# A hybrid encoder layer on one Trainium2 core: the end of mixing in another order, the first gathers inside it, the second expert's loads behind them, the first low part on VectorE, and constant products in TensorE's waits

## The reference, cut to what matters

```
h = concat([meta, x])                       # 16 meta rows + 1024 rows, D = 1024
u = rmsnorm(h);  z = u @ w_in
mixed = concat([rwkv7_mix(z_a), retention_mix(z_b)])
h = h + mixed @ w_out
u = rmsnorm(h, norm_ffn)
# hier_moe(u):
group = top1(softmax(u @ w_rg + b_rg))                  # 4 groups
e1, e2 = top2(softmax(u @ w_re + b_re)[group])          # 8 experts in a group
row_tok[dest] = token of each slot, expert by expert, blocks of 128 rows
for each block (xb = u[row_tok], e):
    hid = silu(xb @ w_gate[e]) * (xb @ w_up[e])         # 1024 -> 512
    y = hid @ w_down[e]                                 # 512 -> 1024
out = rmsnorm(h + weighted sum of the two y rows of a token)
```

## Time and profile before

| what | value |
|---|---|
| median of 3 runs | 1520.82 us (1520.25 to 1533.48) |
| the profiled execution's own time | 1519.76 us |
| its span, first to last instruction | 1517.8 us |
| TensorE busy | 1395.5 us, 92% |
| VectorE busy | 1037.2 us, 68% |
| ScalarE busy | 707.8 us, 47% |
| GpSimd busy | 576.0 us, 38% |
| mean granted TensorE clock | 0.968 |
| read from HBM, written | 295.47 MB, 68.98 MB |

### The profile page before, as it was taken

One profiled execution on the slowest core, in us unless ns is written; L12 is line 12 of the kernel. 1 busy time (PEld: TensorE's weight loads), 2 busy tenths in 40 slices (PEclk: granted clock), 3 DMA queues, 4 the chain that ended last, 5 costly groups with the idle time before them and its releaser, 6 DMA issues. The chain is left out here.

```text
span 1517.8 us, 33023 instructions
## 1 busy us (share of the span) xinstructions
PE 1395.5 (92%) x14368; PEld 1235.1 (81%) x14368; DVE 1037.2 (68%) x1184; ACT 707.8 (47%) x695; POOL 576.0 (38%) x203
## 2 busy tenths in 40 slices
PE   5999999999999899999999749999999999999990
PEld 5989899999988789888898637888888888888870
DVE  5456655544203866776767558999899898777757
ACT  5533442212212412212122137777777777777752
POOL 2001101000000300000000058777877878999985
PEclk9999999999998999999999869999999999999995
DMA  5136555643418324434242369999999999999968
GB/s 211 57 126 189 166 163 165 207 129 112 128 57 279 109 87 134 127 108 141 74 133 72 115 255 423 409 405 407 407 411 404 409 403 410 413 414 414 412 245 324
DMA packets 125369, 366.26 MB, mean 241 GB/s; under 512 B 11680, under 2 KB 79264, under 8 KB 113200
## 3 DMA queue, kind: packets, MB, share of 16 engines
q1 hardware_dynamic: 112432, 318.34, 56.5%
q0 software_dynamic: 6912, 25.17, 4.8%
q10 hardware_dynamic: 5904, 20.97, 3.4%
HBM read 295.47 MB, written 68.98 MB: 240 GB/s over the span
## 5 line engine op out<-in xcount | busy, mean ns | idle before, releaser
L1111 PE MATMUL ps<-u_hi,w_hi 128*128 128x352 f32 (+1 forms) x720 | 237.9, 330 | 4.9 <-DVE u_lo L761 4.9
L1111 PE MATMUL ps<-u_lo,w_hi 128*128 128x352 f32 (+1 forms) x720 | 233.7, 325 | 0.0
L1111 PE MATMUL ps<-u_hi,w_lo 128*128 128x352 f32 (+1 forms) x720 | 232.7, 323 | 0.0
L2534 POOL TENSOR_TENSOR down_lo<-down_raw,down_hi 128x1024 fp32r<-128x1024 f32 x31 | 150.9, 4869 | 62.2 <-ACT down_hi L2603 62.2
L2534 POOL TENSOR_TENSOR gate_lo<-gate_raw,gate_hi 128x1024 fp32r<-128x1024 f32 x32 | 161.3, 5040 | 23.1 <-ACT gate_hi L2603 23.1
L2701 DVE TENSOR_TENSOR down_lo<-down_raw,down_hi 128x3072 fp32r<-128x3072 f32 x31 | 125.6, 4050 | 41.8 <-ACT down_hi L2603 41.8
L1111 PEld LDWEIGHTS ps<-u_hi,w_hi 128*128 128x128 f32 x720 | 137.4, 191 | 11.8 <-issue 5.8
L2701 DVE TENSOR_TENSOR gate_lo<-gate_raw,gate_hi 128x3072 fp32r<-128x3072 f32 x32 | 130.7, 4084 | 14.6 <-ACT gate_hi L2603 14.3
L2701 DVE TENSOR_TENSOR up_lo<-up_raw,up_hi 128x3072 fp32r<-128x3072 f32 x32 | 128.6, 4017 | 15.1 <-ACT up_hi L2603 14.8
L1501 POOL TENSOR_TENSOR mix_stat<-mix_stat,minus_half 128x4 f32<-128x4 f32 x8 | 8.2, 1025 | 341.2 <-DVE mix_stat L1800 341.2
L1111 PEld LDWEIGHTS ps<-u_hi,w_lo 128*128 128x128 f32 x720 | 137.4, 191 | 0.0
(11 more groups left out here) (444 smaller groups left out, 3120.8 us busy)
## 6 DMA issues: line engine op xcount, KB each, us to landing
down_raw<-in_moe_w_down SPq DMA_DIRECT2D x32, 2048.0 KB, 10.9
gate_raw<-in_moe_w_gate SPq DMA_DIRECT2D x31, 2048.0 KB, 10.5
up_raw<-in_moe_w_up SPq DMA_DIRECT2D x31, 2048.0 KB, 9.6
tm_rows<-tm_stage SPq DMA_DIRECT2D x32, 512.0 KB, 3.5
y_slots<-y_out ACTq DMA_DIRECT2D x31, 512.0 KB, 11.5
w_raw<-in_w_in SPq DMA_DIRECT2D x30, 512.0 KB, 4.1
tm<-tm_rows SPq DMA_DIRECT2D x36, 256.0 KB, 3.2
y_slots<-zero SPq DMA_DIRECT2D x15, 512.0 KB, 5.3
```

Source lines behind the costliest of these rows:

```text
L1111: mm = pe.matmul(z_of(n, r_), w[n % 3][:, k_, :], a[:, k_, c0:c1], start=(k_ == 0 and i == 0), stop=(k_ == KD - 1 and i == 2))
L2534: pool.tensor_tensor(lo[e % 2][:, cut:, :], raw[e % 2][:, cut:, :], hi[:, cut:, :].bitcast(F32), ALU.subtract).then_inc(sem(f"{name}_lo2_r ...
```

## The change

All edits are in the mixing block's tail, at the head of the experts' block, and in TensorE's waits within the experts' products.

```diff
+KEPT = ("consts_loaded", "x_rows_loaded0", "x_rows_loaded1", "w_gate_loaded1")   # not cleared
+        second_raw = [... offset=weights_at + (2 + i) * MATRIX ...]   # gate, up of expert 1
+        first_gate_lo = ... offset=weights_at     # in the bytes of first_raw[0]
+        first_gate_hi = ... offset=weights_at + 6 * MATRIX
+        first_x = [... offset=weights_at + 9 * MATRIX + b * 4 * D ...]
# mixing, SyncE, the end
                 first_weights(0, "moe_w_gate")
                 first_weights(1, "moe_w_up")
-                store_h2(NTX)
-                store_u2(NTX)
+                sp.wait_ge(sem("proj1_done"), NTX)
+                sp.wait_ge(sem("proj0_done"), NTX)
                 sp.wait_ge(sem("h2_stored"), 16 * NTX)
                 sp.wait_ge(sem("u2_stored"), 16 * NTX)
+                sp.wait_ge(sem("x_rows_loaded0"), 16)
+                sp.dma_start(second_raw[0][:], d["moe_w_gate"][1]).then_inc(sem("w_gate_loaded1"), 16)
# mixing, GpSimd, the end
                 rstd_h(NTX)
+                pool.wait_ge(sem("u2_stored"), 16 * NTX)
+                pool.wait_ge(sem("slot_row_ready"), 1)
+                for b in range(2):
+                    pool.indirect_dma_start(first_x[b][:], ... slot_row[:, b:b + 1] ...)
# mixing, ScalarE, the end
                 mean_square(NTX)
+                act.dma_start(h2_dram[...], h2[:]).then_inc(sem("h2_stored"), 16)
+                act.wait_ge(sem("first_weights_loaded"), 16 * 4)
+                act.wait_ge(sem("proj1_done"), NTX)
+                act.activation(first_gate_hi[:], first_raw[0][:], ACT.Copy).then_inc(sem("first_gate_hi_ready"), 1)
+                act.wait_ge(sem("u2_ready"), NTX)
+                act.dma_start(u2_dram[...], u2[:]).then_inc(sem("u2_stored"), 16)
# mixing, VectorE: a_gate for all tiles
+                    dve.wait_ge(sem("tm_gate_loaded"), 16 * n)
+                    tt(y[:], y[:], toks(n, "gate"), ALU.mult, "a_gated")
                     dve.wait_ge(sem("rstd_a"), n)
                     tt(heads(y[:]), heads(y[:]), per_head(stat[:, 2, :]), ALU.mult, "a_normed")
                     dve.wait_ge(sem("a_normed"), n)
-                    dve.wait_ge(sem("tm_gate_loaded"), 16 * n)
-                    tt(y[:], y[:], toks(n, "gate"), ALU.mult, "a_gated")
# mixing, VectorE, the end
                 a_variance(NTX)
-                choose_group(NTX - 1)
                 a_gate(NTX)
                 low_a(NTX)
+                choose_group(NTX - 1)
                 choose_first(NTX - 1)
                 choose_second(NTX - 1)
                 residual(NTX, 0)
-                rows(NTX - 2, 0)
+                residual(NTX, 1, LAST_HALF)
+                rows(NTX - 2, ROWS_BANK)
                 ranks(NTX - 1, 0)
                 entries(NTX - 1)
-                rows(NTX - 1, 0)
-                residual(NTX, 1)
                 h_variance(NTX)
-                norm(NTX)
                 logits_of(NTX)
                 choose_group(NTX)
                 choose_first(NTX)
                 choose_second(NTX)
+                norm(NTX)
+                rows(NTX - 1, ROWS_BANK)
                 ranks(NTX, 0)
                 entries(NTX)
-                rows(NTX, 0)
-                dve.tensor_copy(slot_row[:, 0:NE], slot_sum[:]).then_inc(sem("slot_row_ready"), 1)
+                dve.tensor_tensor(slot_row[:, 0:NE], slot_sum[:], ps[:, ROWS_BANK, 128:128 + NE], ALU.add).then_inc(sem("slot_row_ready"), 1)
                 (count copied, slot_row_ready 2 waited for)
+                dve.wait_ge(sem("first_gate_hi_ready"), 1)
+                dve.tensor_tensor(first_gate_lo[:], first_raw[0][:], first_gate_hi[:].bitcast(F32), ALU.subtract)
# mixing, TensorE, the end
                 ret_rows_0(NTX)
+                ret_rows_1(NTX, LAST_HALF)        # ends with keep_busy(..., 2) for tile 8
                 turn_y(NTX)
                 rwkv_rows_0(NTX)
+                rwkv_rows_1(NTX, LAST_HALF)
+                turn_h2_0(NTX)                    # waits for the first half of h2 only
+                rows_of(NTX - 2, ROWS_BANK)
                 rank(NTX - 1, 0)
-                rows_of(NTX - 2, 0)
-                ret_rows_1(NTX)
-                rows_of(NTX - 1, 0)
-                rwkv_rows_1(NTX)
-                turn_h2(NTX)
+                turn_h2_1(NTX)
                 route(NTX)                        # waits for h2_t1 only ahead of its matmul 4 of 8
+                rows_of(NTX - 1, ROWS_BANK)
+                keep_busy(pe, ps, cst, 4, 4)
                 rank(NTX, 0)                      # its count product now behind its other two
+                keep_busy(pe, ps, cst, 4, 1)
-                rows_of(NTX, 0)
+                rows_of(NTX, ROWS_BANK)
+                keep_busy(pe, ps, cst, 4, 6)
# experts, SyncE, the start
-                    sp.wait_ge(sem("x_rows_loaded0"), 16)
-                    sp.dma_start(gate_raw[1][:], one(wg_v, 1))...
+                    for name in ("gate_hi_ready", "gate_lo_ready", "gate_lo2_ready"):
+                        sp.sem_inc(sem(name), 1)
+                    sp.dma_start(down_raw[0][:], one(wd_v, 0))...
                     sp.dma_start(up_raw[1][:], one(wu_v, 1))...
-                    for b in range(2):
-                        sp.dma_start(down_raw[b][:], one(wd_v, b))...
+                    sp.dma_start(down_raw[1][:], one(wd_v, 1))...
# experts, GpSimd, the start
-                    bring_x(0)
-                    bring_x(1)
-                    low("gate", 0)
# experts, ScalarE: high("gate", 0, 0) gone; VectorE: low("gate", 0, 0) gone, turned_x(0) first
# experts, TensorE
-                        pe.wait_ge(sem("gate_lo2_ready"), e + 1)      # ahead of gate(e)
+                        rest = (GATE_CUT, lambda: pe.wait_ge(sem("gate_lo2_ready"), e + 1))
+                        # the same wait, now inside the product, ahead of k = 6 of 8
+                        # up: the same; down, last_down: ahead of k = 3 of 4 of the first half
                     turn_x(0, 0)
+                    keep_busy(pe, ps, env["cst"], 3, 2)
```

More of the change, by code:

```diff
@@ L169, in free_sems @@
         def free_sems():
-            names = [n for n in sems if n != "consts_loaded"]
+            names = [n for n in sems if n not in KEPT]
             nc.clear_and_free_semaphores([sems.pop(n) for n in names])
@@ L1281, in project @@
     return first_at, fm1, m_fm
+LAST_HALF = 1
+COUNT_BANK, ROWS_BANK = 2, 3
+GATE_CUT, DOWN_CUT = 6, 3
 def mix(nc, d, env):
@@ L2092, in m_state, with project @@
                     mm.then_inc(sem("m_products_done"), 1)
-                def project(c, hi, lo, at_, first, last):
+                def project(c, hi, lo, at_, first, last, bank=None):
                     cols = slice(c * 512, (c + 1) * 512)
@@ L2409, in dispatch_and_experts @@
             down_hi_last = nc.alloc_sbuf_tensor_at("down_hi_last", [P, KE, D], F32R, offset=h_at)
-            matrices = {"gate": (gate_raw, gate_lo, gate_hi, 6), "up": (up_raw, up_lo, up_hi, 6),
-                        "down": (down_raw, down_lo, down_hi, 3)}
-            x_rows = [sb(f"x_rows{b}", D) for b in range(2)]
+            matrices = {"gate": (gate_raw, gate_lo, gate_hi, GATE_CUT), "up": (up_raw, up_lo, up_hi, GATE_CUT),
+                        "down": (down_raw, down_lo, down_hi, DOWN_CUT)}
+            assert h_at == rows_at + 6 * MATRIX and nc.sbuf_base == rows_at + 9 * MATRIX
+            sb("first_rows", 2, D)
+            x_rows = env["first_x"]
             x_hi, x_lo = (tile(s, n, [P, KD, P], F32R) for n in ("x_hi", "x_lo"))
@@ L2832, in extra_rows @@
                         dve.wait_ge(sem("extra_rows_ready"), 1)
+                    turned_x(0)
                     weights_begun()
-                    low("gate", 0, 0)
-                    turned_x(0)
                     for e in range(NE):
@@ L2947, in last_down, with down @@
                     def last_down(e, b):
-                        for name in ("hid_hi", "hid_lo", "down_hi", "down_lo", "down_lo2"):
+                        for name in ("hid_hi", "hid_lo", "down_hi", "down_lo"):
                             pe.wait_ge(sem(f"{name}_ready"), e + 1)
-                        product(0, x_hi, x_lo, down_hi_last, down_lo[b], KE, slice(0, 512)).then_inc(sem("last_half_done"), 1)
+                        rest = (DOWN_CUT, lambda: pe.wait_ge(sem("down_lo2_ready"), e + 1))
+                        product(0, x_hi, x_lo, down_hi_last, down_lo[b], KE, slice(0, 512), rest).then_inc(sem("last_half_done"), 1)
                         product(1, x_hi, x_lo, down_hi_last, down_lo[b], KE, slice(512, D)).then_inc(sem("down_done"), 1)
-                    def down(e, b, between=None):
+                    def down(e, b, between=None, whole=False):
                         pe.wait_ge(sem("hid_hi_ready"), e + 1)
@@ L2994, in more @@
                         turn_x(e, 0)
-                        gate(e, 0)
-                        up(e, 0)
+                        gate(e, 0, whole=True)
```

(3 more changed lines are left out.)

96 lines of the change are left out of this document (61 added, 35 removed).

## The result

| | median us | runs | ratio to before, 95% interval |
|---|---|---|---|
| before | 1525.25 (1520.25 to 1533.48) | 10 | |
| after | 1513.81 (1509.04 to 1517.60) | 10 | 0.9926 [0.9910, 0.9943] |

The change is 0.74% faster; the forecast was 1512.0 us in 1504 to 1517, 0.6% faster. The profiled execution of after took 1514.83 us, its span is 1513.0, its mean clock 0.976.

What follows compares the result with a forecast made beforehand. TensorE sets the pace once the experts run, so the start of up(2), fed by mixing's tail and the weights' stream, counts: 1519.76 - 8.8 = 1511.0, plus 1.1 to the median gives 1512.0 us, range 1504 to 1517.

Steps and rivals of the forecast that it cites:

- Part 1: Mixing's tail: slot list at 873.1 and count at 873.3, against 882.0 and 882.18; the tail 8.9 us shorter.
- rival C: Mixing's tail stays at half clock in part, giving 5.5 to 6.5 us; 1514.5 to 1516 us; chance 0.13.
- The gate factor: Mixing's tail: computed ahead of the power -1/2, it was booked at 0.15 us, bounds 0 and 0.7.
- Part 2: Mixing's end: first gather held behind VectorE's low-part subtraction, landing at 882.3; stream of weights 7.3 us earlier; chance 0.50.
- Rival A: Mixing's end: gather ahead of the subtraction, landed 878.0, stream 11.6 us earlier; 1507.7 us; chance 0.28.
- The block's end: End of mixing: waits for SyncE; with 2.0 us of barrier the experts' block begins at 884.7.
- Part 3: Expert 0's first product: gate(0) at 889.5 instead of 894.09, taking 5.6 instead of 7.3 us, done 6.2 earlier.
- Down 0 ahead of up 1: SyncE's queue of loads: up 1 lands third, at about 900, costing nothing, at most 1 us.
- Part 4: Third expert: gate matrix 2 lands at 916.5, GpSimd's quarter no longer counts, up(2) at 930.7, 8.8 us earlier.
- The same rhythm: Experts from up(2) on: unchanged rhythm of 18 us per expert.
- Part 5: Moved waits in the experts' loop: gain nothing, satisfied waits cost nothing; bounds 0 and 0.12 us each.
- rival D: Experts' loop: 31 x 3 waits inside products at 0.12 us each cost 11.2, making 1523.2 us; chance 0.03.

Runs made afterwards that it cites:

- one gather: The changed kernel with only the first gather issued in mixing, the second first on GpSimd in the experts' block; 1512.60 us, ratio 0.9918.
- the first experiment: The changed kernel with the low part of the first gate matrix back at the head of the experts' block; 1509.18 us, ratio 0.9895.
- up 1 first: The changed kernel with up matrix 1 requested ahead of down matrix 0 again; 1511.42 us, ratio 0.9917.

## Why the prediction was right, and where its terms were off

The sign and the mechanism were right: a shorter tail and a stream of weights that starts earlier. That the time came within 2 us is partly luck. The prediction took 8.8 us off 1520.8, the median of three runs of before; ten runs gave 1525.25, 4.4 us more, and the change gained 11.4 by the medians and 7.1 to 7.4 behind y0. As a ratio it told 0.9942, just inside the interval of 0.9910 to 0.9943. The prediction's own times are put behind y0 here by taking 845.17 off.

- **Part 1, the tail.** Forecast 8.9 us shorter with the count at 28.1; measured 29.0 after and in two kernels more, 27.4 in seven with the same tail. The two values are some eight rwkv matmuls at half clock, or none, with the same instructions ahead: rival C in small, at 1.6 us and not the 2.5 and more that it was priced at. "I take full clock from here on" was right in seven of ten profiles. The gate factor gave 0.42 us (turn at 6.91 against 7.33), not 0.15.
- **Part 2, gather second.** Held, by the forecast's mechanism: subtraction 4.43 (4.5 forecast), gather ending 1.01 behind it (0.9), landing 3.4 later (3.5), gate matrix 1 requested at 37.9 (37.1). What was called a choice "by a hair" was none: the prediction let the gather start as soon as list and store were there, but it started 0.77 us behind the count and never earlier in the other eight profiles, the subtraction 0.03; in all five with the subtraction in mixing it was held, for 4.46 to 4.70 us. The store, which was to decide, landed 0.07 us ahead of the list in after; where it landed 0.8 behind it (one gather) the gather was only later. Rival A's condition came in none of them. That it was priced nearly right the first experiment shows: with the subtraction away, gate matrix 1 goes at 33.4 (A: 32.8), up(2) at 80.2 (A: 81.2). The Trainium skill ("SBUF — State Buffer", section "Who interferes with whom") infers that descriptor generation needs only the write side; the pair of 4.70 with and 1.14 without the subtraction speaks against that for these gathers. The section's rule that issue order decides who blocks agrees with the gather; with the 7.36 us of down_lo it agrees only for GpSimd's first subtraction, as the second began 1.72 us behind VectorE's and still went ahead of it.
- **The block's end: the step that failed.** "The block's end waits for SyncE; with the 2.0 us of barrier ... the experts' block begins at 884.7", 39.5 behind y0. It began at 42.1. SyncE was at the barrier at 38.4, but GpSimd was last, at 40.1, waiting for the landing of its second gather, a wait that the prediction put at nothing. Gate(0) came at 46.6 instead of 44.3.
- **Part 3, gate(0).** Half clock only for its first matmuls, 6.0 us for 5.6 booked. Down 0 ahead of up 1: 0.8 us by one profile, inside the scatter, booked 0 to 1.
- **Part 4, up(2).** Gate matrix 2 landed at 72.5 (71.3 forecast), up(2) started at 86.7 (85.5): 7.7 us earlier, not 8.8. From the request of gate matrix 1 to the landing of gate matrix 2 it took 34.6 us, 34.2 booked, so the late block seems to matter little for it, and the error of 2.3 us at gate(0) shrank to 1.2. Settled it isn't: only gate matrix 1 is requested from mixing, and "one gather", whose request goes when that of "up 1 first" goes (36.2 and 36.4) but whose block opens 1.7 us sooner, has gate matrix 2 landed 1.5 us sooner (68.6 against 70.1). The wait for GpSimd's quarter that Part 4 took away from gate(2) is the right term for before (its end at 933.0, gate(2) at 933.1); with the waits put back, the quarter of up(0) is what costs.
- **Behind up(2).** "The same rhythm" was nearly right. The wait of 1.3 us at down(1) was not foreseen; it is gone when the waits are put back, so it is a price of the moved waits in the first experts.
- **Part 5** was right as a sum (0 forecast, 0.5 us by the profile, nothing by the ratio), and rival D fell: the 93 waits inside products cost nothing that shows (end 665.6 with them, 666.1 with the waits ahead).
- **The size over the whole.** Behind y0 the change gives 7.1 to 7.4 us, by the medians 11.4 with an interval of 8.7 to 13.7 (0.9 to 0.57% of 1525). The rest lies ahead of y0, or is scatter. Three edits act there in every step of mixing: the gate factor, which alone gave 0.9996, and the later waits of `turn_h2` and `route`, which no run tried alone. The scatter ahead of y0 is large: VectorE's last addition into y of tile 1 ends at 515.6 to 516.6 us in five of the fourteen profiles and at 520.5 to 521.9 in nine, and the kernel before has one of either. Medians of one kernel differed by 4 us; whether anything real is in this rest stays open.

## What to carry to other kernels

A step that is moved ahead of a barrier belongs to the barrier: here each gather pulled into the block in front had to land before that block could end, and the six filler products were waited for too. Before filling an idle engine, look which engine's work the new piece takes turns with: a 4.4 us subtraction, placed where VectorE had nothing else to do, held a 1.1 us gather and cost some 5 us to save 0.3, because the gather began the chain. And try the parts alone: behind y0 the new tail with the moved waits gave 9.9 us, the whole change 7.1, the change without its first low part 14.4, of which 1.6 is the clock.

## What the runs showed of the hardware

- GpSimd's instruction at the end of a block lasted 10.08 us, until its two gathers had landed; in nine profiles it ended 0.08 to 0.13 us behind the last landing. "Block" less "issue" is 2.0 to 2.1 without a gather (and without the six products), 5.6 to 5.7 with one, 6.1 to 6.5 with two.
- The first gather starts 0.87 or 0.88 us behind the end of the slot list in seven profiles (0.77 or 0.78 behind the count); in two more, where the store of `u2` landed 0.65 and 0.83 us behind the list, it starts 0.29 behind that landing. A VectorE instruction starts 0.03 behind the count that it waits for: of the two engines VectorE is first, although its signal comes 0.10 us later.
- Held work isn't slowed in proportion, it waits for its turn: VectorE's 3.36 us became 7.36 when two of GpSimd's subtractions (2.41 and 2.42) followed each other without a gap, the second of them begun behind VectorE's.
- TensorE's clock in the tail went either of two ways with the same instructions, in ten profiles: full speed in seven, half for eight matmuls in three, behind idle times of only 0.68 and 1.50 us.
